# Two fused transformer blocks on one core: halved tiles and a leading VectorE tile around the second feed-forward block

## The chip, the cores and the metric

The kernel runs on one core of one Trainium2 chip. The metric is the device time of one execution in microseconds (us). Differences under about 0.2% (6.4 us) can't be told from no change with this kernel.

## The reference, cut to what matters

Two transformer blocks run one after the other over 1,024 tokens of width 1,024, all in f32. The second one ends so (the rest of both blocks isn't touched by the change):

```python
def rmsnorm(x, g):
    xf = x.astype(jnp.float32)
    y = xf * lax.rsqrt(jnp.mean(xf * xf, axis=-1, keepdims=True) + EPS)
    return (y * g.astype(jnp.float32)).astype(x.dtype)

def modulate(h, shift, scale):
    return h * (1 + scale) + shift

def swiglu(h, w_gu, w_down):
    a, b = jnp.split(h @ w_gu, 2, axis=-1)
    return (jax.nn.silu(a) * b) @ w_down

# in second_block; D_MODEL 1024, D_FF_2 2816
x = x + mx[2] * (jnp.concatenate([att_x, hg_x], axis=-1) @ w_out[l])
x = x + mx[5] * swiglu(modulate(rmsnorm(x, g_norm2[l]), mx[3], mx[4]), w_gu[l], w_down[l])
...
return rmsnorm(x, g_final)
```

## The kernel before

**Data.** Activations lie feature-major: `m["x"]` is 8 tiles (`KT`) of 128 features x 1,024 tokens. Every large product is split for accuracy: an operand is kept as a rounded high part (`b_hi` for activations, `whi` for weights) and a remainder (`b_lo`, `wlo`), and a product takes three matmuls: high x high, high x remainder, remainder x high. A matmul takes 512 tokens, so one input tile k into one output tile is 6 matmuls (`gemm_piece`, L512), and 48 for an output tile over all 8 input tiles. Four PSUM regions of 128 x 1,024 (`psl[0]` to `psl[3]`) are used: 0 to 2 in turn for outputs, 3 for column sums, and 2 also for the row of normalizing factors (the token row).

**Order.** Each engine runs its own program, in the written order, and waits on counters of named events: `up(name, ...)` marks an event and `at(name, ...)` waits for it. P, A, V and G are the counters of TensorE (PE), ScalarE (ACT), VectorE (DVE) and GpSimd (POOL). The counters `wh`, `ww` and `gm` say that a weight unit's high part is made, that its remainder is made, and that a unit's product is done. Weights are loaded by DMA from SP, rounded by ACT (L493) and subtracted by DVE (L501), three buffers of each.

**The stretch in question, stage "p".** `pe_project` makes the 8 output tiles of `w_out`. DVE adds each of them, times its gate, to the residual (L1486). ACT squares the new tile (L1433), POOL adds the squares of tiles 0 to 6 into `acc` (L1402), and `pe_stat` sums the columns of `acc` and then of the last square with a matrix of ones (L86). All engines then wait for those sums (`after_project`). Next, in `act_mlp` and `dve_mlp`, one more weight unit is split (L493, L501), DVE scales the sums (L1705), ACT takes the root (L1625), DVE the reciprocal (L1707), and PE turns the result into the token row by 8 transposes (`rows`, L79).

**The eight input tiles.** For each k in order, DVE makes z = x times the column factor times the token row (L1713), ACT adds the shift and rounds it to `b_hi` (L1632), and DVE makes the remainder `b_lo` (L1716). z has two buffers, the squares' buffers `m["sq"]`. PE waits for the event `l` k and then does 12 matmuls for that k: 6 for each of the first two units of `w_gu`. From the third unit on, PE has whole units of 48 matmuls. `mlp_plan` orders the 22 pairs of up tiles (`w_gu`) and the six groups of down tiles (L1604).

**Stage "d", the last group.** The same add (L1763), square and sum follow the last group of down tiles, which has two input tiles: 12 matmuls for each of 8 output tiles. Then `dve_last` scales (L2701), takes the reciprocal (L2703), and multiplies the eight tiles by gain and token row (L2707), and `sp_last` stores each of them to HBM (L2684).

Of the kernel before, what the change touches and what calls it, by code (L numbers as in the profile page):

```python
# [15 lines left out]
T = 1024  # L16
TC = 256
TA = T + TC
KT = 8
# [27 lines left out]
class Signal:  # L47
# [23 lines left out]
    def end(self):  # L71
        return self.sem, self.step if self.known is None else max(self.known.values())

# [255 lines left out]
class Kernel:  # L329
# [1024 lines left out]
    def after_project(self, e, sig):  # L1354
        e.wait_ge(*sig[0].at("cs", "p", KT - 1))
        e.wait_ge(*sig[1].at("sq", "p", KT - 1))
        e.wait_ge(*sig[2].at("add", KT - 1))
# [29 lines left out]
    def pe_stat(self, e, m, sig, tag):  # L1387

        P, A, V, G = sig
        e.wait_ge(*G.at("acc", tag, KT - 2))  # L1390
        col_sums(e, self.psl[3], m["acc"], self.con("ones"), True, False)
        e.wait_ge(*A.at("sq", tag, KT - 1))
        col_sums(e, self.psl[3], m["sq"][(KT - 1) % 2], self.con("ones"), False, True).then_inc(*P.up("cs", tag, KT - 1))
# [40 lines left out]

    def act_project(self, e, m, sig, name):
        P, A, V, G = sig
        j0 = UNIT[name, 0]
        for i in range(KT):
            if i:
                self.act_weights(e, j0 + i + 3)  # L1440
            if i:
                e.wait_ge(*V.at("add", i - 1))
                self.act_stat(e, m, sig, "p", i - 1, m["x"][:, i - 1, :])
        first = name == "dn_out"
        for k in range(KT - 1 if first else 0):
            e.wait_ge(*P.at("taken", k))
            self.act_plain(e, m, sig, k)
        e.wait_ge(*V.at("add", KT - 1))
        if first:
            e.wait_ge(*self.gm.at(j0 + KT - 1))  # L1450
            self.act_plain(e, m, sig, KT - 1)
        self.act_stat(e, m, sig, "p", KT - 1, m["x"][:, KT - 1, :])
        if not first:
            self.after_project(e, sig)
# [11 lines left out]
    def dve_project(self, e, m, sig, name, gate=None):  # L1466
        P, A, V, G = sig
        j0 = UNIT[name, 0]
        for i in range(KT):
# [13 lines left out]
            if gate is None:  # L1483
                e.tensor_tensor(x, x, ps, ALU.add).then_inc(*V.up("add", i))
            else:
                e.scalar_tensor_tensor(out=x, in0=ps, scalar=gate[i], in1=x, op0=ALU.mult,  # L1486
                                       op1=ALU.add).then_inc(*V.up("add", i))
# [43 lines left out]
    def pe_mlp(self, e, m, sig, n_ff, ring, up, down, beside=None):  # L1531
# [5 lines left out]
        def tokens():  # L1537
            e.wait_ge(*V.at("rc"))
            rows(e, self.psl[2], self.st[:, 0:8], self.con("ident")).then_inc(*P.up("rw"))

        if gated:
            tokens()
            for k in range(KT):
                e.wait_ge(*V.at("l", k))
                for part in range(2):
                    for i in range(2):
                        if k == 0 and part == 0:
                            e.wait_ge(*self.ww.at(j0 + i))
                        ins = self.gemm_piece(e, self.psl[i], j0 + i, k, part, self.b_hi, self.b_lo)
                        if k == KT - 1 and part == 1:  # L1550
                            ins.then_inc(*self.gm.up(j0 + i))
# [67 lines left out]
    def act_mlp(self, e, m, sig, n_ff, ring, up, down, shift=None, beside=None):  # L1619
# [6 lines left out]
        if shift is None:  # L1626
            e.wait_ge(*P.at("rw"))
            e.activation(m["row"], self.psl[2], ACT.Copy).then_inc(*A.up("row"))
        else:
            for k in range(KT):  # L1630
# [5 lines left out]
        for kind, f, n in mlp_plan(n_ff, ring):  # L1636
# [31 lines left out]
            else:  # L1668
                for i in range(8):
# [5 lines left out]
                    if f + n == n_ff and i:  # L1675
                        for k in (i - 1, 7) if i == 7 else (i - 1,):
                            e.wait_ge(*V.at("down", f, k))
# [20 lines left out]

    def dve_mlp(self, e, m, sig, n_ff, ring, up, down, wcol, shift=None, gate=None, beside=None):
# [8 lines left out]
        e.wait_ge(*P.at("rw") if gated else A.at("row"))  # L1708
        for k in range(KT if gated else 0):
            z = m["sq"][k % 2]  # L1710
            if k >= 2:
                e.wait_ge(*V.at("l", k - 2))
            e.scalar_tensor_tensor(out=z, in0=m["x"][:, k, :], scalar=wcol[:, k:k + 1], in1=self.psl[2],  # L1713
                                   op0=ALU.mult, op1=ALU.mult).then_inc(*V.up("z", k))
            e.wait_ge(*A.at("h", k))
            e.scalar_tensor_tensor(out=self.b_lo[:, k, :], in0=z, scalar=shift[:, k:k + 1],  # L1716
                                   in1=self.b_hi[:, k, :].bitcast(F32), op0=ALU.add, op1=ALU.subtract).then_inc(*V.up("l", k))
        j = j0 + 2
        before = {}
        for kind, f, n in mlp_plan(n_ff, ring):  # L1720
# [27 lines left out]
            else:  # L1748
                for i in range(8):
# [12 lines left out]
                    else:  # L1762
                        e.scalar_tensor_tensor(out=x, in0=ps, scalar=gate[i], in1=x, op0=ALU.mult,  # L1763
                                               op1=ALU.add).then_inc(*V.up("down", f, i))
# [915 lines left out]
    def sp_last(self, e):  # L2680
        V = self.mm2[2]
        for k in range(KT):
            e.wait_ge(*V.at("y", k))
            e.dma_start(self.out[:, k, :], self.x2[:, k, :]).then_inc(*self.outst.up(k))  # L2684
        e.wait_ge(*self.outst.end())

    def pe_last(self, e):
        P, A, V, G = self.mm2
        e.wait_ge(*V.at("rc2"))
        rows(e, self.psl[2], self.st[:, 0:8], self.con("ident")).then_inc(*P.up("rw2"))  # L2690
# [7 lines left out]
    def dve_last(self, e):  # L2698
# [5 lines left out]
        e.wait_ge(*P.at("rw2"))  # L2704
        for k in range(KT):
            x = self.x2[:, k, :]
            e.scalar_tensor_tensor(out=x, in0=x, scalar=self.par("gf")[:, k:k + 1], in1=self.psl[2], op0=ALU.mult,  # L2707
                                   op1=ALU.mult).then_inc(*V.up("y", k))

# [478 lines left out]
```

## Time and profile before

| | before |
|---|---|
| median of 3 runs | 3191.41 us (3189.16 to 3192.23) |
| the profiled execution, its own time | 3190.96 us |
| its span, first to last instruction | 3189.1 us |
| mean granted clock of PE, share of full | 0.987 |
| PE busy | 3046.8 us (96%) |
| DVE, ACT, POOL busy | 1543.6, 1000.1, 450.3 us (48%, 31%, 14%) |
| DMA, mean over the span | 58 GB/s |

The table says which engine is busy, and not which one sets the end of a stretch. For that the chain of waits and the timeline of the stretch are read. PE's clock is granted at one of two levels, 2.4 GHz (1.00 in the windows) and 1.2 GHz (0.50).

### The profile page before, as it was taken

How to read it: one execution, taken by the hardware profiler on the slowest of the kernel's cores; microseconds unless marked ns; L12 is line 12 of the kernel's file. 1: busy time of each engine (PE TensorE's matmuls, PEld its weight loads, DVE VectorE, ACT ScalarE, POOL GpSimd, SP SyncE). 2: the span in 40 equal slices, each digit the busy share in tenths (PEclk: the TensorE clock that was granted, in tenths of full speed). 3: DMA queues.
4: the chain of work that ended last, by engine and by line, in shares of the span. 5: the costliest groups of instructions: out<-in, count | busy, mean ns of one | idle time of the engine just before them, and what ended most of it. 6: DMA issues, size and time to landing. Idle time of an engine off the chain costs nothing.

```text
span 3189.1 us, 36113 instructions
## 1 busy us (share of the span) xinstructions
PE 3046.8 (96%) x14927; PEld 2487.1 (78%) x14927; DVE 1543.6 (48%) x1907; ACT 1000.1 (31%) x1441; POOL 450.3 (14%) x352
## 2 busy tenths in 40 slices
PE   8899999989999999999989999999898999999997
PEld 6688888878788888888866668888776888888886
DVE  7566666553565553433566764456644122222224
ACT  5555555552311122212423332233322111111111
POOL 4333333321000001000300002133300000000001
PEclk9999999999999999999999999999999999999999
DMA  3111111122233431111210001101131111111111
GB/s 124 40 47 47 47 47 47 47 67 99 65 115 121 129 120 52 49 51 47 94 54 7 9 10 48 34 21 40 47 112 31 56 47 47 52 47 47 50 43 60
DMA packets 77235, 184.75 MB, mean 58 GB/s; under 512 B 7056, under 2 KB 29072, under 8 KB 77072
## 3 DMA queue, kind: packets, MB, share of 16 engines
q1 hardware_dynamic: 77072, 182.44, 18.2%
q8 instruction: 119, 1.95, 0.3%
q14 instruction: 44, 0.36, 0.0%
HBM read 163.87 MB, written 15.79 MB: 56 GB/s over the span
## 4 chain that ended last, share of the span: by engine, by line
PE 86%; DVE 8%; ACT 4%; issue 2%; POOL 0%; DMA 0%; POOLq 0%; DVEq 0%; SPq 0%; ACTq 0%
PE ps L512 39%; PE ps L1604 18%; PE ps L2950 8%; PE ps L2291 4%; DVE b L2899 2%; PE ps L2429 1%; PE ps L909 1%; PE ps L2255 1%; PE ps L2284 1%; PE ps L2283 1%; DVE b L501 1%; PE ps L916 1%; ACT b L493 1%; PE ps L86 1%; PE ps L891 1%
## 5 line engine op out<-in xcount | busy, mean ns | idle before, releaser
L512 PE MATMUL ps<-b 128*128 128x512 f32 x6024 | 1494.9, 399 | 35.6 <-DVE b L501 14.0
L512 PEld LDWEIGHTS ps<-b 128*128 128x128 f32 x6024 | 1109.9, 190 | 251.2 <-issue 19.9
L1604 PE MATMUL ps<-b 128*128 128x512 f32 x2592 | 599.1, 392 | 0.7 <-DVE b L1745 0.7
L1604 PEld LDWEIGHTS ps<-b 128*128 128x128 f32 x2592 | 485.0, 187 | 109.3 <-DVE b L1745 1.1
L501 DVE TENSOR_TENSOR b<-b 128x1024 fp32r<-128x1024 f32 (+1 forms) x206 | 255.3, 1241 | 288.3 <-ACT b L493 280.9
L493 ACT ACTIVATE b<-b 128x1024 fp32r<-128x1024 f32 (+1 forms) x206 | 214.9, 1045 | 515.9 <-PE ps L1604 427.4
L2950 PE MATMUL ps<-b 128*128 128x512 f32 (+1 forms) x1464 | 327.3, 379 | 6.8 <-ACT b L3010 5.9
L2950 PEld LDWEIGHTS ps<-b 128*128 128x128 f32 x1464 | 255.0, 192 | 56.5 <-issue 11.5
L1402 POOL TENSOR_TENSOR b<-b 128x1024 f32<-128x1024 f32 x18 | 43.2, 2399 | 916.8 <-ACT b L1433 916.4
L2291 PE MATMUL ps<-b 128*128 128x512 f32 x320 | 163.0, 592 | 0.0
L1761 DVE TENSOR_TENSOR b<-b,ps 128x1024 f32<-128x1024 f32 x64 | 78.1, 1220 | 152.4 <-PE ps L1604 152.3
L2301 ACT ACTIVATE b<-ps 128x512 f32<-128x512 f32 x160 | 95.3, 597 | 149.7 <-PE ps L2284 149.7
L1763 DVE SCALAR_TENSOR_TENSOR b<-ps,b 128x1024 f32<-128x1024 f32 x48 | 61.6, 1283 | 150.2 <-PE ps L1604 150.2
L1665 ACT ACTIVATE b<-b 128x1024 fp32r<-128x1024 f32 x54 | 57.3, 1060 | 217.2 <-DVE b L1736 216.2
L2313 DVE TENSOR_REDUCE b<-ps 128x1 f32<-128x1280 f32 x64 | 95.1, 1488 | 42.7 <-PE ps L2255 42.3
L1661 ACT ACTIVATE b<-b 128x1024 f32<-128x1024 f32 x32 | 33.9, 1060 | 251.8 <-DVE b L1741 251.8
L1745 DVE TENSOR_TENSOR b<-b 128x1024 fp32r<-128x1024 f32 x54 | 66.2, 1225 | 95.8 <-ACT b L1665 95.8
L1741 DVE SCALAR_TENSOR_TENSOR b<-ps,b 128x1024 f32<-128x1024 f32 x32 | 39.2, 1224 | 148.1 <-PE ps L512 135.9
L1238 POOL TENSOR_TENSOR b<-b 128x256 f32<-128x256 f32 x96 | 82.7, 864 | 194.4 <-DVE b L1126 115.6
L1736 DVE TENSOR_TENSOR b<-b,ps 128x1024 f32<-128x1024 f32 x22 | 26.9, 1222 | 165.9 <-PE ps L512 162.2
L2899 DVE SCALAR_TENSOR_TENSOR b<-b 128x1024 f32<-128x1024 f32 x72 | 104.4, 1450 | 0.8
L2283 PE MATMUL ps<-b 128*128 128x512 f32 x160 | 98.5, 616 | 0.0
(306 smaller groups left out, 3292.8 us busy)
## 6 DMA issues: line engine op xcount, KB each, us to landing
b<-in_down SPq DMA_DIRECT2D x52, 512.0 KB, 3.7
b<-in_mod SPq DMA_DIRECT2D x96, 256.0 KB, 2.7
b<-in_gu SPq DMA_DIRECT2D x44, 512.0 KB, 3.6
b<-scratch SPq DMA_DIRECT2D x38, 512.0 KB, 4.4
b<-in_dn_in SPq DMA_DIRECT2D x32, 512.0 KB, 5.1
b<-in_up SPq DMA_DIRECT2D x32, 512.0 KB, 3.8
b<-in_win SPq DMA_DIRECT2D x26, 512.0 KB, 3.7
scratch<-b SPq DMA_DIRECT2D x18, 512.0 KB, 2.9
```

What stands on the lines that cost most here:

```text
L493: e.activation(self.whi[j % SPL][:, 0:cols], self.raw[j % RAW][:, 0:cols], ACT.Copy).then_inc(*self.wh.up(j))
L501: e.tensor_tensor(self.wlo[j % SPL][:, 0:cols], self.raw[j % RAW][:, 0:cols], self.whi[j % SPL][:, 0:cols].bitcast(F32), ALU.subtract).the ...
L512: ins = e.matmul(ps[:, c], w, h[:, k, c], start=first and k == 0 and i == 0, stop=last and k == KT - 1 and i == 2)
L1238: e.tensor_tensor(out, own, m.broadcast_to([128, 4, 64 >> lv, 1 << lv]), ALU.mult).then_inc(*G.up("m", h, lv, f))
L1604: ins = e.matmul(ps[:, c], w, u[:, at[k], c], start=k == 0 and p == 0, stop=k == n - 1 and p == 2)
L1761: e.tensor_tensor(x, x, ps, ALU.add).then_inc(*V.up("down", f, i))
L2283: e.matmul(S[t % 3], blk(self.ks[g], b), self.qs[g][:, :, qc], start=True, stop=False)
L2291: e.matmul(O[i % 2], self.vx[:, b, 64 * g:64 * g + 128], self.prob[(t - 2) % 4], start=b == 0, stop=b == 9).then_inc(*P.up("pv", t - 2))
L2301: e.activation(self.prob[t % 4], S[t % 3], ACT.Exp, scale=0.125).then_inc(*A.up("ex", t))
L2313: e.tensor_reduce(mx[:, j:j + 1], MX[1 if i else j % 2], AX.X, ALU.max).then_inc(*V.up("mx", i, j))
L2899: e.scalar_tensor_tensor(out=dst, in0=k.d_pad[c % 2][:, t:t + T], scalar=cw[:, t:t + 1], in1=dst, op0=ALU.mult, op1=ALU.add).then_inc(*V.u ...
L2950: ins = e.matmul(self.bank[p], (hi, hi, lo)[i], x, start=k == 0 and i == 0, stop=last)
```

## The change

`HALVES` are tokens 0 to 511 and 512 to 1,023. Outside the second feed-forward block and its two borders nothing changes. The first block's calls of the same helpers keep their form.

- The last residual tile, k = 7, of the stages "p" and "d" is added in two halves, squared in two halves (`act_stat_last`), and its column sums are two sets of four.
- The token row is made in two halves, each with its own event.
- Input tile 0 is made in halves throughout: z, high part, remainder, and PE's first 12 matmuls in two sets of six.
- In `dve_first_tiles`, DVE makes z for tile k + 1 ahead of the remainder of tile k, after a wait for the remainder of tile k - 1, which frees the buffer.
- At the end the token row is made in halves, the final multiplies of tiles 0 and 7 are halves, and tile 7 is stored as two DMAs.

The diff:

```diff
@@ -70,6 +70,10 @@
 
     def end(self):
         return self.sem, self.step if self.known is None else max(self.known.values())
+
+
+
+HALVES = (slice(0, 512), slice(512, 1024))
 
 
 def rows(e, ps, cols, ident):
@@ -1353,8 +1357,9 @@
 
     def after_project(self, e, sig):
         e.wait_ge(*sig[0].at("cs", "p", KT - 1))
-        e.wait_ge(*sig[1].at("sq", "p", KT - 1))
-        e.wait_ge(*sig[2].at("add", KT - 1))
+        half = [1] if sig is self.mm2 else []
+        e.wait_ge(*sig[1].at("sq", "p", KT - 1, *half))
+        e.wait_ge(*sig[2].at("add", KT - 1, *half))
 
     def pe_project(self, e, m, sig, name, free):
 
@@ -1389,8 +1394,15 @@
         P, A, V, G = sig
         e.wait_ge(*G.at("acc", tag, KT - 2))
         col_sums(e, self.psl[3], m["acc"], self.con("ones"), True, False)
-        e.wait_ge(*A.at("sq", tag, KT - 1))
-        col_sums(e, self.psl[3], m["sq"][(KT - 1) % 2], self.con("ones"), False, True).then_inc(*P.up("cs", tag, KT - 1))
+        sq = m["sq"][(KT - 1) % 2]
+        if m is self.m1:
+            e.wait_ge(*A.at("sq", tag, KT - 1))
+            col_sums(e, self.psl[3], sq, self.con("ones"), False, True).then_inc(*P.up("cs", tag, KT - 1))
+            return
+        for f, c in enumerate(HALVES):
+            e.wait_ge(*A.at("sq", tag, KT - 1, f))
+            ins = col_sums(e, self.psl[3][:, c], sq[:, c], self.con("ones"), False, True, 4)
+        ins.then_inc(*P.up("cs", tag, KT - 1))
 
     def pool_stat(self, e, m, sig, tag):
 
@@ -1431,6 +1443,15 @@
         if k >= 2:
             e.wait_ge(*G.at("acc", tag, max(1, k - 2)))
         e.activation(m["sq"][k % 2], x, ACT.Square).then_inc(*A.up("sq", tag, k))
+
+    def act_stat_last(self, e, m, sig, tag, made):
+
+        P, A, V, G = sig
+        k = KT - 1
+        e.wait_ge(*G.at("acc", tag, k - 2))
+        for f, c in enumerate(HALVES):
+            e.wait_ge(*made[f])
+            e.activation(m["sq"][k % 2][:, c], m["x"][:, k, c], ACT.Square).then_inc(*A.up("sq", tag, k, f))
 
     def act_project(self, e, m, sig, name):
         P, A, V, G = sig
@@ -1445,12 +1466,13 @@
         for k in range(KT - 1 if first else 0):
             e.wait_ge(*P.at("taken", k))
             self.act_plain(e, m, sig, k)
-        e.wait_ge(*V.at("add", KT - 1))
         if first:
+            e.wait_ge(*V.at("add", KT - 1))
             e.wait_ge(*self.gm.at(j0 + KT - 1))
             self.act_plain(e, m, sig, KT - 1)
-        self.act_stat(e, m, sig, "p", KT - 1, m["x"][:, KT - 1, :])
-        if not first:
+            self.act_stat(e, m, sig, "p", KT - 1, m["x"][:, KT - 1, :])
+        else:
+            self.act_stat_last(e, m, sig, "p", [V.at("add", KT - 1, f) for f in range(2)])
             self.after_project(e, sig)
 
     def act_plain(self, e, m, sig, k):
@@ -1483,8 +1505,9 @@
             if gate is None:
                 e.tensor_tensor(x, x, ps, ALU.add).then_inc(*V.up("add", i))
             else:
-                e.scalar_tensor_tensor(out=x, in0=ps, scalar=gate[i], in1=x, op0=ALU.mult,
-                                       op1=ALU.add).then_inc(*V.up("add", i))
+                for f, c in enumerate(HALVES if i == KT - 1 else [slice(0, T)]):
+                    e.scalar_tensor_tensor(out=x[:, c], in0=ps[:, c], scalar=gate[i], in1=x[:, c], op0=ALU.mult,
+                                           op1=ALU.add).then_inc(*V.up("add", i, *([f] if i == KT - 1 else [])))
         if gate is None:
             self.dve_plain(e, m, sig, KT - 1)
         else:
@@ -1536,16 +1559,23 @@
 
         def tokens():
             e.wait_ge(*V.at("rc"))
-            rows(e, self.psl[2], self.st[:, 0:8], self.con("ident")).then_inc(*P.up("rw"))
+            for f, c in enumerate(HALVES):
+                rows(e, self.psl[2][:, c], self.st[:, 4 * f:4 * f + 4], self.con("ident")).then_inc(*P.up("rw", f))
 
         if gated:
             tokens()
-            for k in range(KT):
+            for f, c in enumerate(HALVES):
+                e.wait_ge(*V.at("l", 0, f))
+                for i in range(2):
+                    if f == 0:
+                        e.wait_ge(*self.ww.at(j0 + i))
+                    a, b = blk(self.whi[(j0 + i) % SPL], 0), blk(self.wlo[(j0 + i) % SPL], 0)
+                    for w, h in ((a, self.b_hi), (a, self.b_lo), (b, self.b_hi)):
+                        e.matmul(self.psl[i][:, c], w, h[:, 0, c], start=w is a and h is self.b_hi, stop=False)
+            for k in range(1, KT):
                 e.wait_ge(*V.at("l", k))
                 for part in range(2):
                     for i in range(2):
-                        if k == 0 and part == 0:
-                            e.wait_ge(*self.ww.at(j0 + i))
                         ins = self.gemm_piece(e, self.psl[i], j0 + i, k, part, self.b_hi, self.b_lo)
                         if k == KT - 1 and part == 1:
                             ins.then_inc(*self.gm.up(j0 + i))
@@ -1624,10 +1654,13 @@
         e.wait_ge(*V.at("ms"))
         e.activation(self.st[:, 8:16], self.st[:, 0:8], ACT.Sqrt).then_inc(*A.up("rt"))
         if shift is None:
-            e.wait_ge(*P.at("rw"))
+            e.wait_ge(*P.at("rw", 1))
             e.activation(m["row"], self.psl[2], ACT.Copy).then_inc(*A.up("row"))
         else:
-            for k in range(KT):
+            for f, c in enumerate(HALVES):
+                e.wait_ge(*V.at("z", 0, f))
+                e.activation(self.b_hi[:, 0, c], m["sq"][0][:, c], ACT.Identity, bias=shift[:, 0:1]).then_inc(*A.up("h", 0, f))
+            for k in range(1, KT):
                 e.wait_ge(*V.at("z", k))
                 e.activation(self.b_hi[:, k, :], m["sq"][k % 2], ACT.Identity, bias=shift[:, k:k + 1]).then_inc(*A.up("h", k))
         group = self.mlp_group(n_ff, ring)
@@ -1674,6 +1707,9 @@
                         next(beside, None)
                     if f + n == n_ff and i:
                         for k in (i - 1, 7) if i == 7 else (i - 1,):
+                            if gated and k == KT - 1:
+                                self.act_stat_last(e, m, sig, "d", [V.at("down", f, k, half) for half in range(2)])
+                                continue
                             e.wait_ge(*V.at("down", f, k))
                             if gated:
                                 self.act_stat(e, m, sig, "d", k, m["x"][:, k, :])
@@ -1695,6 +1731,33 @@
             if kind == "down" and i == f:
                 return (n + m) % 3
             n += (2 if gated else 1) if kind == "up" else 8
+
+    def dve_first_tiles(self, e, m, sig, wcol, shift):
+
+        P, A, V, G = sig
+
+        def tile(k, c):
+            return e.scalar_tensor_tensor(out=m["sq"][k % 2][:, c], in0=m["x"][:, k, c], scalar=wcol[:, k:k + 1],
+                                          in1=self.psl[2][:, c], op0=ALU.mult, op1=ALU.mult)
+
+        def low(k, c):
+            return e.scalar_tensor_tensor(out=self.b_lo[:, k, c], in0=m["sq"][k % 2][:, c], scalar=shift[:, k:k + 1],
+                                          in1=self.b_hi[:, k, c].bitcast(F32), op0=ALU.add, op1=ALU.subtract)
+
+        for f, c in enumerate(HALVES):
+            e.wait_ge(*P.at("rw", f))
+            tile(0, c).then_inc(*V.up("z", 0, f))
+        for f, c in enumerate(HALVES):
+            e.wait_ge(*A.at("h", 0, f))
+            low(0, c).then_inc(*V.up("l", 0, f))
+            if f == 0:
+                tile(1, slice(0, T)).then_inc(*V.up("z", 1))
+        for k in range(1, KT):
+            if k + 1 < KT:
+                e.wait_ge(*V.at("l", k - 1, *([1] if k == 1 else [])))
+                tile(k + 1, slice(0, T)).then_inc(*V.up("z", k + 1))
+            e.wait_ge(*A.at("h", k))
+            low(k, slice(0, T)).then_inc(*V.up("l", k))
 
     def dve_mlp(self, e, m, sig, n_ff, ring, up, down, wcol, shift=None, gate=None, beside=None):
         P, A, V, G = sig
@@ -1705,16 +1768,10 @@
         e.tensor_scalar(self.st[:, 0:8], self.psl[3][:, 0:1024:128], 1.0 / D, EPS, ALU.mult, ALU.add).then_inc(*V.up("ms"))
         e.wait_ge(*A.at("rt"))
         e.reciprocal(self.st[:, 0:8], self.st[:, 8:16]).then_inc(*V.up("rc"))
-        e.wait_ge(*P.at("rw") if gated else A.at("row"))
-        for k in range(KT if gated else 0):
-            z = m["sq"][k % 2]
-            if k >= 2:
-                e.wait_ge(*V.at("l", k - 2))
-            e.scalar_tensor_tensor(out=z, in0=m["x"][:, k, :], scalar=wcol[:, k:k + 1], in1=self.psl[2],
-                                   op0=ALU.mult, op1=ALU.mult).then_inc(*V.up("z", k))
-            e.wait_ge(*A.at("h", k))
-            e.scalar_tensor_tensor(out=self.b_lo[:, k, :], in0=z, scalar=shift[:, k:k + 1],
-                                   in1=self.b_hi[:, k, :].bitcast(F32), op0=ALU.add, op1=ALU.subtract).then_inc(*V.up("l", k))
+        if gated:
+            self.dve_first_tiles(e, m, sig, wcol, shift)
+        else:
+            e.wait_ge(*A.at("row"))
         j = j0 + 2
         before = {}
         for kind, f, n in mlp_plan(n_ff, ring):
@@ -1760,8 +1817,10 @@
                     if gate is None:
                         e.tensor_tensor(x, x, ps, ALU.add).then_inc(*V.up("down", f, i))
                     else:
-                        e.scalar_tensor_tensor(out=x, in0=ps, scalar=gate[i], in1=x, op0=ALU.mult,
-                                               op1=ALU.add).then_inc(*V.up("down", f, i))
+                        halves = f + n == n_ff and i == KT - 1
+                        for half, c in enumerate(HALVES if halves else [slice(0, T)]):
+                            e.scalar_tensor_tensor(out=x[:, c], in0=ps[:, c], scalar=gate[i], in1=x[:, c], op0=ALU.mult,
+                                                   op1=ALU.add).then_inc(*V.up("down", f, i, *([half] if halves else [])))
                     if beside:
                         next(beside, None)
 
@@ -2680,14 +2739,16 @@
     def sp_last(self, e):
         V = self.mm2[2]
         for k in range(KT):
-            e.wait_ge(*V.at("y", k))
-            e.dma_start(self.out[:, k, :], self.x2[:, k, :]).then_inc(*self.outst.up(k))
+            for f, c in enumerate(HALVES if k == KT - 1 else [slice(0, T)]):
+                e.wait_ge(*V.at("y", k, f))
+                e.dma_start(self.out[:, k, c], self.x2[:, k, c]).then_inc(*self.outst.up(k, f))
         e.wait_ge(*self.outst.end())
 
     def pe_last(self, e):
         P, A, V, G = self.mm2
         e.wait_ge(*V.at("rc2"))
-        rows(e, self.psl[2], self.st[:, 0:8], self.con("ident")).then_inc(*P.up("rw2"))
+        for f, c in enumerate(HALVES):
+            rows(e, self.psl[2][:, c], self.st[:, 4 * f:4 * f + 4], self.con("ident")).then_inc(*P.up("rw2", f))
 
     def act_last(self, e):
         P, A, V, G = self.mm2
@@ -2701,12 +2762,15 @@
         e.tensor_scalar(self.st[:, 0:8], self.psl[3][:, 0:1024:128], 1.0 / D, EPS, ALU.mult, ALU.add).then_inc(*V.up("ms2"))
         e.wait_ge(*A.at("rt2"))
         e.reciprocal(self.st[:, 0:8], self.st[:, 8:16]).then_inc(*V.up("rc2"))
-        e.wait_ge(*P.at("rw2"))
         for k in range(KT):
-            x = self.x2[:, k, :]
-            e.scalar_tensor_tensor(out=x, in0=x, scalar=self.par("gf")[:, k:k + 1], in1=self.psl[2], op0=ALU.mult,
-                                   op1=ALU.mult).then_inc(*V.up("y", k))
-
+            for f, c in enumerate(HALVES if k in (0, KT - 1) else [slice(0, T)]):
+                if k == 0:
+                    e.wait_ge(*P.at("rw2", f))
+                x = self.x2[:, k, c]
+                ins = e.scalar_tensor_tensor(out=x, in0=x, scalar=self.par("gf")[:, k:k + 1], in1=self.psl[2][:, c], op0=ALU.mult,
+                                             op1=ALU.mult)
+                if k or f:
+                    ins.then_inc(*V.up("y", k, f if k else 0))
 
 
     def sync_program(self, e):
```

## Rows read from the trace of the kernel before

**Rows 1.** The page's chain that ended last, shares of the span by engine

```profile
PE 86%; DVE 8%; ACT 4%; issue 2%; POOL 0%; DMA 0%; POOLq 0%; DVEq 0%; SPq 0%; ACTq 0%
```

**Rows 2.** Chain from stage "p" on: start us, us, engine and line

```profile
2425.09 2.07 PE ps L86 x16
...
2430.20 1.10 PE ps L79 x8
...
2435.11 1.20 DVE b L1713
...
2436.33 1.16 ACT b L1632
...
2437.51 1.28 DVE b L1716
2438.80 1.20 DVE b L1713
...
2461.04 111.82 PE ps L512 x492
...
2617.66 87.06 PE ps L512 x384
```

**Rows 3.** Timeline of the same stretch; in brackets the idle time before

```profile
2422.39 1.95 PE L86 MATMUL ps<-b 128*128 128x128 f32 x16
2422.66 1.28 DVE L1486 SCALAR_TENSOR_TENSOR b<-ps,b 128x1024 f32<-128x1024 f32 x1 [7.27 <-PE ps L512]
...
2431.33 1.28 DVE L1713 SCALAR_TENSOR_TENSOR b<-b,ps 128x1024 f32<-128x1024 f32 x1 [1.18 <-PE ps L79]
...
2435.16 10.41 PE L512 MATMUL ps<-b 128*128 128x512 f32 x36 [3.87 <-DVE b L1716]
...
2468.20 2.35 DVE L501 TENSOR_TENSOR b<-b 128x1024 fp32r<-128x1024 f32 x2
```

**Rows 4.** Windows: busy us (count) of PE, PEld, DVE, ACT, POOL; clock; DMA

```profile
2431.70:2435.16 3.46, 0.00 (x0) 0.00 (x1) 2.24 (x3) 1.15 (x1) 0.00 (x0) 0.51 0.22 90
2435.16:2438.50 3.34, 3.34 (x8) 2.66 (x9) 2.12 (x2) 1.15 (x1) 0.00 (x0) 0.50 0.00 0
...
688.50:694.00 5.50, 5.18 (x16) 4.22 (x17) 2.30 (x5) 0.93 (x3) 0.72 (x1) 0.50 0.66 186
854.50:858.30 3.80, 3.49 (x8) 2.79 (x9) 2.53 (x3) 1.21 (x2) 0.00 (x0) 0.55 0.66 185
2350.50:2356.50 6.00, 5.85 (x18) 5.01 (x19) 1.91 (x3) 0.60 (x1) 0.00 (x0) 0.50 0.59 202
```

**Rows 5.** Groups by shape, half tiles of the stage before: busy us, mean ns

```profile
L2659 DVE SCALAR_TENSOR_TENSOR b<-b 128x512 f32<-128x512 f32 x2 | 1.5, 751 | 0.1
L1338 ACT ACTIVATE b<-b 128x512 fp32r<-128x512 f32 x2 | 1.3, 630 | 3.7 <-DVE b L2659 3.7
```

**Rows 6.** Timeline of DVE: L1486 waits for DVE's own L1476

```profile
2355.82 1.28 DVE L1476 SCALAR_TENSOR_TENSOR b<-b,ps 128x1024 f32<-128x1024 f32 x1 [3.99 <-DMA b<-scratch]
2357.14 1.28 DVE L1486 SCALAR_TENSOR_TENSOR b<-ps,b 128x1024 f32<-128x1024 f32 x1
```

**Rows 7.** Timeline of stage "d" and the end

```profile
3167.20 2.35 POOL L1402 TENSOR_TENSOR b<-b 128x1024 f32<-128x1024 f32 x1 [0.34 <-ACT b L1433]
...
3168.86 1.06 ACT L1433 ACTIVATE b<-b 128x1024 f32<-128x1024 f32 x1 [1.74 <-DVE b L1763]
...
3169.60 3.84 PE L86 MATMUL ps<-b 128*128 128x128 f32 x32 [2.09 <-POOL b L1402]
...
3174.18 1.09 PE L79 MATMUL ps<-b 128*128 128x128 f32 x8 [0.74 <-DVE b L2703]
3175.30 9.62 DVE L2707 SCALAR_TENSOR_TENSOR b<-b,ps 128x1024 f32<-128x1024 f32 x8 [1.18 <-PE ps L79]
3176.61 8.67 SPq L2684 DMA_DIRECT2D out<-b  x8
```

**Rows 8.** Window of the last stores, columns as in rows 4

```profile
3177.50:3187.50 10.00, 0.00 (x0) 0.00 (x0) 7.42 (x7) 0.00 (x0) 0.00 (x0) 0.59 1.02 405
```

## The prediction

> **What bounds the kernel now.** I read four views in this order. The page's chain of waits says that PE is the chain for 86% of the span, DVE for 8% and ACT for 4% [rows 1]. So an edit to DVE or ACT is worth something only where the chain leaves PE, and the change touches three such places.
>
> The chain in order of time shows the first two [rows 2]. At 2425.09 PE starts its last column sums, which take 2.07 us, to 2427.16. At 2430.20 the token row starts, and then a ladder begins: DVE makes z, ACT the high part, DVE the remainder, and the next z starts where the last one did plus 3.69 us (2435.11 to 2438.80). PE is in the chain again only from 2461.04. From there it has no break: 384 matmuls in 87.06 us are 0.2267 us each, so the 12 for one input tile take 2.72 us. PE needs 2.72, the ladder gives a tile every 3.69, and PE idles for the difference. The timeline shows which engine had been ready: PE had finished the first sums at 2424.34 (2422.39 + 1.95) and waited for the last square [rows 3].
>
> The third place is the end. There the timeline shows POOL's last sum ending at 3169.55, PE's 32 matmul records following without a gap, and the stores trailing the final multiplies [rows 7]. The windows show the stores running at 405 GB/s with the DMA engines full [rows 8].
>
> **Part 1, stage "p" by halves.** A half add costs 0.75 alone and a half square about 0.63, from the half tiles of the stage before [rows 5]. A whole op starts 1.20 after a whole op in front of it though it lasts 1.28 [rows 2], so I let a second half start 0.67 after the first. First half: 2422.66 + 0.75 + 0.63 + two handovers of 0.03 gives 2424.10. PE is in the first sums until 2424.34, so it doesn't wait. Second half: the add ends at 2422.66 + 0.67 + 0.75 = 2424.08, the square at 2424.74, and PE wants it near 2425.3. PE thus runs all 32 records in one piece. Stage "d" has that piece: 3.84 us [rows 7]. 2422.39 + 3.84 = 2426.23 against 2427.16 is **0.93 us gained**. If the pipeline has to fill twice (1.95 + 2.05) it is 0.77. The way from the sums to the token row (3.04 us) has the same instructions as before and moves with it.
>
> **Part 2, the eight tiles.** I count from the start of the token row, which was 2430.20. Before, PE took up tile 7 at 2461.04, or 30.84, and left it at 30.84 + 2.72 = **33.56**. For the changed order:
>
> - Eight transposes take 1.09 and z starts at 1.13 [rows 2, 3, 7]. Four end half of 1.09 sooner, near 0.58, and z starts at 0.62.
> - z half 0 ends at 1.37, half 1 starts at 1.28 and ends at 2.03. A half high part I put at 0.72 (0.63 plus the 0.09 by which a whole one, 1.16, exceeds a whole square, 1.06) [rows 2, 5, 7]. The halves end at 2.11 and 2.83.
> - Remainder half 0 ends at 2.13 + 0.75 = 2.88, and PE starts at 2.94. z of tile 1 starts at 2.79, remainder half 1 at 3.99, ends 4.74. PE is busy with half 0 until about then at full clock, longer at the lower one.
> - z of tile 2 waits for that remainder and starts at 4.77, remainder 1 at 5.97, and ends at 7.25. PE can start tile 1 at 7.31.
> - From there DVE's period is a z that waited for DVE's own last result and a remainder behind it: 1.32 (2355.82 to 2357.14) [rows 6] plus 1.20 is 2.52 us. ACT's 1.16 lies beside DVE's remainder. 2.52 is under PE's 2.72, so PE sets the pace.
>
> If PE's clock were full, the end would be 7.31 + 7 x 2.72 = 26.35. But PE starts at the lower level. Before, it fell to 0.50 about 4.5 us after the sums and stayed there for the first 3.34 us of work; a matmul then took 3.34 / 8 = 0.42 us [rows 4]. The ladder hid that, since tile 0 had 3.69 us of slack behind it and every next tile 0.97 more. Now nothing hides it beyond the wait for tile 1. With C us of work at the lower level the end is 2.94 + 96 x 0.2267 + C x (1 - 0.2267 / 0.42) = 24.70 + 0.46 C, and never below 26.35. Four stretches of dense work show C: 3.34, 3.4 (3.8 us at a mean of 0.55), 5.5 and 6.0 [rows 4]. I take their mean, 4.6, because where the clock rises within new work can't be read from a stretch that starts elsewhere. The end is 26.8, and the gain **33.56 - 26.8 = 6.76 us**, with 7.21 at C = 3.3 and 6.10 at C = 6.0.
>
> The Trainium skill, "TensorE: Matmul & The Clock Gate", Part 1, says that the clock is low by default, is released by sustained work, and that the same kernel can show different counts of slow matmuls from run to run. The four stretches agree as far as they go. Its durations for 512 columns, 426.7 and 215.7 ns, would make the factor 0.49 in place of 0.46 and the end, by an estimate, 0.15 us later.
>
> Behind tile 7 nothing else is due. The fourth unit's remainder was ready at 2469.4 (first of the two at 2468.20) [rows 3], while PE asks for it one unit of 48 matmuls after 2463.76, at 2474.6. That split hangs on the first unit's product, so it moves with PE and keeps its 5.2 us. SP's weight loads keep their order and their waits.
>
> **Part 3, stage "d" by halves.** I cost it at nothing. The last square ended at 3169.92, and PE began only at 3169.60, when POOL was done, with 1.92 us of other sums first [rows 7]. The cover for the two extra half instructions is that 1.6 us. Without it an extra half pair would cost 0.1 to 0.2.
>
> **Part 4, the end.** z of tile 0 starts at 3174.18 + 0.62 = 3174.80 in place of 3175.30. Its second half ends at 3174.80 + 0.66 + 0.75 = 3176.21, where the whole tile ended at 3176.58. The first store goes out 0.37 sooner. From there the stores set the end: 8 tiles are 4.19 MB, at 405 GB/s 10.4 us [rows 8], while DVE needs 9.62 for all eight tiles [rows 7], so they fall behind DVE and the end follows the first store. **0.37 us gained.** Halving the last store moves no bytes off the queue. I bound its effect by minus 0.2 (a ninth issue; eight spanned 8.67 us) and plus 0.65 (half of one tile's 1.3 us, if the queue were empty), and take 0.
>
> The Trainium skill, "DMA: Bandwidth & Descriptors", Rules for kernel authors, advises against splitting a transfer in two, because both parts use the same 16 engines. It speaks of partition halves and these are column halves; the full engines in the window agree. Its "Perfetto Trace Analysis", DMA Optimizations, expects splitting to help when the engines are idle, which would give the 0.65.
>
> **Sum.** 0.93 + 6.76 + 0 + 0.37 = 8.06 us. Against the profiled execution's own time, 3190.96, that is 3182.90. The median of the runs is 0.45 above it, so 3183.4, or 0.25% faster.
>
> **Rivals.**
>
> - *The clock stays low.* If short waits between tiles kept PE at the lower level through all 96 matmuls, the end would be 2.94 + 96 x 0.42 = 43.3, 9.7 later than before, and the total 3191.4 + 9.7 - 1.3 = 3199.8. It decides from C = 22 us of work on. Against it: in this same stretch the clock rose after 3.34 us of work, at a lower density of work than is to come, and the longest low stretch of dense work is 6.0 [rows 4]. Chance 0.03. The same page of the Trainium skill warns, in its section on HAM oscillation, of matmul bursts between waits that leave the clock low each time; the ladder of before doesn't show it.
> - *DVE's lead doesn't come about,* because the wait for its own remainder or the shared buffers put z, high part and remainder in a row again. Then tile 7 is ready at 7.25 + 6 x 3.69 = 29.39, PE ends it at 32.17, and the gain is 1.39 + 0.93 + 0.37 = 2.7: 3188.7. From a period of 2.80 on, DVE would be the bound. For it: each z does wait for DVE's own result. Against it: that wait is in rows 6 and costs 0.12. Chance 0.07.
> - *Only the eight tiles bring anything, and at the slow end:* the borders are swallowed by another wait and C is 6.0. Then 6.1 are gained: 3185.3. For it: in both borders the first consumer is a queue or a pooled sum that another engine feeds. Chance 0.08.
> - *Nothing gained or a small loss elsewhere,* for example from code that now lies otherwise in a program of 3,100 other microseconds: 3191. Nothing in the rows speaks for it. Chance 0.02.
>
> **How the numbers follow.** The forecast has 0.80. Its own working spans 0.77 + 6.10 + 0.17 = 7.0 to 0.93 + 7.21 + 1.02 = 9.2 us, or 3182.2 to 3184.4. The runs of before lie 2.3 below to 0.8 above their median. Together that is 3181 to 3186; I set the upper end at 3186.5 for the third rival. The line for "faster" is 3185.0. Most of the forecast's 0.80 is above that gain, with 0.02 more from the third rival: 0.79. Slower has the first rival's 0.03. The rest, 0.18, is within 0.2%.
>
> **What would show it.** In stage "p" PE's sums are one piece of 32 records of about 3.84 us. The ladder's chain goes from DVE and ACT to PE after tile 1, DVE's z starts lie about 2.7 apart (held by nothing but its own order, 2.5), and the 96 matmuls take 24 to 25 us from first to last. In stage "d" the sums still follow POOL. The last store lands 0.4 us sooner relative to the sums. The prediction is wrong if PE shows waits between tiles 2 to 7, if the clock is low for over 8 us of work, or if a wait appears at the third or fourth unit.

## The result and the profile after

| | before | changed |
|---|---|---|
| median of 17 runs each | 3192.31 us (3189.16 to 3196.28) | 3183.52 us (3180.83 to 3189.33) |
| ratio, with 95% interval | | 0.9975 (0.9969 to 0.9982) |
| profiled span | 3189.1 us | 3180.9 us |

The changed kernel is 0.25% faster; the interval, 0.18 to 0.31%, begins just under the 0.2% that count. The forecast was 3183.4 us. The kernel before came out at 3192.31, 0.9 us above the median of three runs, 3191.41, from which the forecast had started. The 17 runs of each kernel fall into a lower and an upper group: ten and seven of before (to 3192.8, from 3194.8), twelve and five of the changed one (to 3184.4, from 3187.8), and the means are 8.1 us apart in the lower group and 7.0 in the upper one.

The chain of waits of the changed kernel, from stage "p" on (start in us, duration in us, engine and line; x32 is a count of instructions):

```profile
2421.10 3.70 PE ps L90 x32
...
2426.01 1.22 DVE b L505
...
2427.84 1.98 PE ps L83 x8
...
2429.85 0.75 DVE b L1740
2430.60 0.70 DVE b L1744
...
2431.34 5.49 PE ps L1574 x12
2436.83 128.07 PE ps L516 x564
```

In [rows 2] DVE and ACT carried the chain for all eight tiles. Now they carry it for less than one: from 2431.34 on the chain is PE without a break. The column sums (x32) are one piece. Two things stand out: the token row took 1.98 us, where before it took 1.10, and the first 12 matmuls took 5.49, where 12 take 2.72 at the full clock.

The timeline of the same stretch shows why DVE left the chain:

```profile
2420.93 3.85 PE L90 MATMUL ps<-b 128*128 128x128 f32 x32
2421.20 1.41 DVE L1509 SCALAR_TENSOR_TENSOR b<-ps,b 128x512 f32<-128x512 f32 x2 [7.27 <-PE ps L516]
...
2431.34 5.49 PE L1574 MATMUL ps<-b 128*128 128x512 f32 x12 [1.53 <-DVE b L1744]
...
2435.69 1.28 DVE L1740 SCALAR_TENSOR_TENSOR b<-b,ps 128x1024 f32<-128x1024 f32 x1
...
2436.89 1.28 DVE L1744 SCALAR_TENSOR_TENSOR b<-b 128x1024 fp32r<-128x1024 f32 x1
2437.00 1.15 ACT L1665 ACTIVATE b<-b 128x1024 fp32r<-128x1024 f32 x1 [1.36 <-DVE b L1740]
2438.20 1.28 DVE L1740 SCALAR_TENSOR_TENSOR b<-b,ps 128x1024 f32<-128x1024 f32 x1
...
2455.68 1.03 ACT L1688 ACTIVATE b<-ps 128x1024 f32<-128x1024 f32 x1 [4.50 <-PE ps L516]
```

One z (L1740) starts 2.51 us after the one before, and ACT's high part (L1665) lies beside DVE's remainder (L1744). No z or remainder has an idle time in front of it. The last line is the first activation of the block. In all ten profiles it starts 0.03 us before the last matmul of tile 7 does. Reckoned as the forecast did it, by 12 x 0.2267 from PE's first matmul for tile 7, the end of tile 7 was 2463.76 in the kernel before and its activation started at 2463.65. So I use this start as the mark in all kernels, and add 0.11 us where I compare with the forecast.

The windows give the reason for 1.98 and 5.49 (columns as in [rows 4]):

```profile
2424.80:2426.90 2.10, 0.00 (x0) 0.00 (x0) 0.89 (x1) 1.06 (x1) 0.00 (x0) 0.98 0.40 115
2426.90:2431.34 4.44, 1.97 (x8) 1.57 (x8) 2.85 (x7) 1.64 (x3) 0.00 (x0) 0.50 0.52 182
2431.34:2437.00 5.66, 5.66 (x13) 4.47 (x14) 5.59 (x6) 2.31 (x3) 0.00 (x0) 0.50 0.00 0
2437.10:2439.00 1.90, 1.90 (x10) 1.54 (x9) 1.86 (x2) 1.06 (x1) 0.00 (x0) 1.00 0.00 0
```

PE's clock fell to 0.50 at 2426.8, two microseconds after the sums. So it was low under the whole token row, and through the first 5.7 us of matmuls.

Stage "d" and the end, on the timeline, answering to [rows 7]:

```profile
3159.23 2.35 POOL L1414 TENSOR_TENSOR b<-b 128x1024 f32<-128x1024 f32 x1 [0.34 <-ACT b L1445]
...
3160.42 1.23 ACT L1454 ACTIVATE b<-b 128x512 f32<-128x512 f32 x2 [1.27 <-DVE b L1822]
3161.63 3.84 PE L90 MATMUL ps<-b 128*128 128x128 f32 x32 [2.10 <-POOL b L1414]
...
3166.21 1.09 PE L83 MATMUL ps<-b 128*128 128x128 f32 x8 [0.74 <-DVE b L2764]
```

POOL releases the sums as before, and the halved squares end at 3161.65, 1.9 us before PE has done its first sixteen sums and comes to them.

**Where the 8.2 us of span went.** I cut both spans at five marks:

| stretch | before | changed | difference |
|---|---|---|---|
| start to the column sums of "p" | 2422.39 | 2420.93 | 1.46 |
| sums to token row | 7.81 | 6.91 | 0.90 |
| token row to first activation | 33.45 | 27.84 | 5.61 |
| first activation to sums of "d" | 705.95 | 705.95 | 0 |
| sums of "d" to last token row | 4.58 | 4.58 | 0 |
| last token row to end of span | 14.92 | 14.69 | 0.23 |

The change itself is worth 6.74 us in this pair. The other 1.46 us come from stages whose instructions are the same in both. The spans are known to 0.1 us, so the last row can be off by 0.05.

### The profile page after: what moved, and what is told of

It is laid out like the page before. It is cut to its first block, busy times and chain, and to the rows that moved or that the text cites. A ratio compares the mean times of both kernels' runs of the same rounds, so it can differ in the third digit from the quotient of the medians.

```text
span 3180.9 us, 36123 instructions
## 1 busy us (share of the span) xinstructions
PE 3044.1 (96%) x14927; PEld 2486.9 (78%) x14927; DVE 1545.2 (49%) x1913; ACT 1001.1 (31%) x1444; POOL 451.3 (14%) x352
## 4 chain that ended last, share of the span: by engine, by line
PE 86%; DVE 7%; ACT 4%; issue 2%; POOL 0%; DMA 0%; POOLq 0%; DVEq 0%; SPq 0%; ACTq 0%
PE ps L516 39%; PE ps L1634 18%; PE ps L3014 8%; PE ps L2350 4%; DVE b L2963 2%; PE ps L2488 1%; PE ps L913 1%; PE ps L2314 1%; PE ps L2343 1%; PE ps L2342 1%; DVE b L505 1%; PE ps L920 1%; PE ps L90 1%; ACT b L497 1%; PE ps L895 1%
## 5 line engine op out<-in xcount | busy, mean ns | idle before, releaser
L1822 DVE SCALAR_TENSOR_TENSOR b<-ps,b 128x1024 f32<-128x1024 f32 (+1 forms) x49 | 61.7, 1261 | 150.2 <-PE ps L1634 150.2
L1798 DVE SCALAR_TENSOR_TENSOR b<-ps,b 128x1024 f32<-128x1024 f32 x32 | 39.2, 1224 | 147.9 <-PE ps L516 135.7
```

## The experiments

Eight kernels were run in two groups, each beside the kernel before. Five of them have one run only, and one total can't tell a part of the change from noise. So the verdicts rest on the stretches, which repeat to 0.05 us where the clock is the same (the last column, rounded as above, to 0.1). No kernel had stage "d" and the end changed alone, so what is said of them is by elimination. C is the time in us for which PE worked at the lower clock from its first matmul for tile 0 on; "hidden" means that the tiles came so slowly that this cost nothing.

| kernel | start of sums | sums to token row | token row to first activation | C | last row to end |
|---|---|---|---|---|---|
| before | 2422.39 | 7.81 | 33.45 | 3.4, hidden | 14.92 |
| changed | 2420.93 | 6.91 | 27.84 | 5.7 | 14.69 |
| lead_alone | 2423.29 | 7.81 | 28.19 | 3.4 | 14.94 |
| tile0_halves_alone | 2427.15 | 7.81 | 32.16 | hidden | 14.93 |
| stage_d_store_whole | 2420.76 | 6.91 | 27.55 | 6.1 | 14.65 |
| pe_kept_busy | 2425.42 | 6.92 | 26.32 | 0 | 14.71 |
| stage_p_alone | 2420.95 | 6.90 | 34.32 | hidden | 15.00 |
| before_kept_busy | 2424.88 | 7.81 | 33.46 | 0 | 14.92 |
| changed_again | 2420.24 | 6.91 | 26.96 | 4.9 | 14.66 |
| busy_in_both_stages | 2421.87 | 6.92 | 26.33 | 0 | 14.71 |

From the first activation to the sums of "d" it was 705.95 to 706.00 in all ten.

**lead_alone.** Against the kernel before:

```diff
+        tile(0, whole).then_inc(*V.up("z", 0))
+        tile(1, whole).then_inc(*V.up("z", 1))
+        low(0, whole)                      # after the high part of tile 0
         for k in range(1, KT):
-            if k >= 2: e.wait_ge(*V.at("l", k - 2))
-            tile(k, whole).then_inc(*V.up("z", k))
+            if k + 1 < KT:
+                e.wait_ge(*V.at("l", k - 1))
+                tile(k + 1, whole).then_inc(*V.up("z", k + 1))
             e.wait_ge(*A.at("h", k))
             low(k, whole).then_inc(*V.up("l", k))
```

> Only DVE's order is changed: z of tile k + 1 ahead of the remainder of tile k, all tiles whole, nothing halved anywhere. My theory: DVE's period falls from 3.69 to 2.51 us, PE starts tile 0 at 4.95 us after the token row (as before) and becomes the bound; from the token row to the end of tile 7 it takes 26.7 + 0.46 C, with C us of work at the lower clock, so 28.2 to 29.5 in place of 33.56: 4 to 5.3 us gained, the largest part of the change. The rival (the halves of tile 0 carry the gain, and the wait for the own remainder keeps the ladder) expects 32 or more.

Its timeline (the line numbers are those of its own kernel, here and below):

```profile
2431.10 1.09 PE L85 MATMUL ps<-b 128*128 128x128 f32 x8 [3.06 <-DVE b L1804]
...
2436.06 6.20 PE L518 MATMUL ps<-b 128*128 128x512 f32 x19 [3.88 <-DVE b L1763]
...
2438.55 1.28 DVE L1759 SCALAR_TENSOR_TENSOR b<-b,ps 128x1024 f32<-128x1024 f32 x1
...
2441.06 1.28 DVE L1759 SCALAR_TENSOR_TENSOR b<-b,ps 128x1024 f32<-128x1024 f32 x1
...
2459.29 1.03 ACT L1707 ACTIVATE b<-ps 128x1024 f32<-128x1024 f32 x1 [5.55 <-PE ps L518]
```

PE starts 4.96 after the token row, the z's are 2.51 apart, and the stretch is 28.19 (28.30 to the end of tile 7). The forecast's formula gives 26.7 + 0.46 x 3.4 = 28.3. The order of DVE alone is worth 5.26 us. The rival, which expected 32 or more, falls.

**tile0_halves_alone.** The kernel before with only the token row and tile 0 by halves. DVE's order is the old one for tiles 1 to 7, as this part of the diff against the changed kernel shows:

```diff
         for k in range(1, KT):
-            if k + 1 < KT:
-                e.wait_ge(*V.at("l", k - 1, *([1] if k == 1 else [])))
-                tile(k + 1, slice(0, T)).then_inc(*V.up("z", k + 1))
+            if k >= 2:
+                e.wait_ge(*V.at("l", k - 2, *([1] if k == 2 else [])))
+            tile(k, slice(0, T)).then_inc(*V.up("z", k))
```

> Only the token row and tile 0 are halved (z, high part, remainder, PE's first twelve matmuls); the ladder for tiles 1 to 7 is the old one. My theory: the ladder keeps its 3.69 us per tile and starts about 1.3 us sooner, so the way from the token row to the end of tile 7 is 32.3 us in place of 33.56, and the lower clock costs nothing. The rival (halves carry the gain) expects 28 or less.

```profile
2445.90 1.27 DVE L1759 SCALAR_TENSOR_TENSOR b<-b,ps 128x1024 f32<-128x1024 f32 x1
...
2449.60 1.27 DVE L1759 SCALAR_TENSOR_TENSOR b<-b,ps 128x1024 f32<-128x1024 f32 x1
```

The timeline has the old 3.70 us from z to z, and the stretch is 32.16: 1.29 gained, and the rival, 28 or less, falls. The two parts add to 6.55. Together they gave 5.6 to 6.5 in the three profiles without idle matmuls, and 33.45 - 26.32 = 7.13 at full clock.

**stage_d_store_whole.** The changed kernel with these two edits undone:

```diff
-                        halves = f + n == n_ff and i == KT - 1
+                        halves = False       # and act_stat whole for k = 7
-            for f, c in enumerate(HALVES if k in (0, KT - 1) else [slice(0, T)]):
+            for f, c in enumerate(HALVES if k == 0 else [slice(0, T)]):
```

> The changed kernel with stage d whole again and the last tile multiplied and stored whole; the last token row and the first tile's final multiply stay halved. My theory: neither mattered. From the first activation of the second feed-forward block to the start of the last sums it takes 705.95 us, as in both kernels, and from the last token row to the end of the span 14.7, as in the changed one. The rival (the halved last store brings the 0.2 us at the end) expects 14.9 as before the change; if the halved square helped, the sums would start 0.2 or more later.

```profile
3160.43 1.06 ACT L1447 ACTIVATE b<-b 128x1024 f32<-128x1024 f32 x1 [1.74 <-DVE b L1856]
3161.17 3.84 PE L92 MATMUL ps<-b 128*128 128x128 f32 x32 [2.10 <-POOL b L1416]
```

The whole square ends at 3161.49, after PE has begun the sums but before it gets to this square, and the sums keep their place and length. The end is 14.65 against 14.69. Neither half brought anything, so the gain at the end is left to the halved token row and first multiply. The stores bear this out:

```profile
3166.44 9.75 DVE L2805 SCALAR_TENSOR_TENSOR b<-b,ps 128x512 f32<-128x512 f32 x9 [0.74 <-PE ps L85]
3167.87 8.68 SPq L2778 DMA_DIRECT2D out<-b  x8
```

The eight stores went out over 8.68 us, as before (8.67), but began 2.12 us after the token row's start at 3165.75, where it was 2.43.

**pe_kept_busy.** The changed kernel with 18 matmuls whose result is overwritten:

```diff
         if gated:
+            self.pe_warm(e, j0, 11)      # 128x512 matmuls of a weight tile into psl[0]
             tokens()
+            self.pe_warm(e, j0, 7)
```

> The changed kernel with 18 idle matmuls on PE, whose result is overwritten: 11 between the sums and the token row, 7 between the token row and tile 0, both in time in which PE waits. My theory: the lower clock is what the changed kernel lost against my forecast, in the token row (1.97 us in place of 1.09) and in the first matmuls. With PE at work the clock stays at 1.00, the token row takes 1.1, and from its start to the end of tile 7 it is 26.4 us in place of 27.95: about 1.5 us off the total, 0.05% against the changed kernel, 0.3% against the one before. The rival (tile 7's end is set by DVE's period and the clock is beside the point) expects 27.9 again.

Timeline and one window:

```profile
2429.03 2.79 PE L1566 MATMUL ps<-b 128*128 128x512 f32 x11
...
2432.34 1.09 PE L85 MATMUL ps<-b 128*128 128x128 f32 x8 [0.52 <-DVE b L1804]
...
2435.37 1.66 PE L1591 MATMUL ps<-b 128*128 128x512 f32 x6 [0.33 <-DVE b L1763]
...
2458.66 1.03 ACT L1707 ACTIVATE b<-ps 128x1024 f32<-128x1024 f32 x1 [3.46 <-PE ps L518]
```

```profile
2430.00:2435.00 5.00, 4.48 (x23) 3.19 (x22) 3.34 (x6) 1.78 (x4) 0.00 (x0) 1.00 0.65 210
```

The clock stays at 1.00, the first six matmuls take 1.66, and the stretch is 26.32 in place of 27.84: 1.52 us, as expected. The ratio of the totals to the kernel before was 0.9976 (0.9966 to 0.9986; ten runs), so the expected 0.05% against the changed kernel isn't seen there. This profile reached the sums at 2425.42, 4.5 us later than the changed one, for a reason that lies ahead of the edit (last section).

**stage_p_alone.** Against the kernel before:

```diff
-                e.scalar_tensor_tensor(out=x, in0=ps, ...).then_inc(*V.up("add", i))
+                for f, c in enumerate(HALVES if i == KT - 1 else [slice(0, T)]): ...
-        self.act_stat(e, m, sig, "p", KT - 1, m["x"][:, KT - 1, :])
+        self.act_stat_last(e, m, sig, "p", [V.at("add", KT - 1, f) for f in range(2)])
```

> Only the add, the square and the column sums of the last residual tile of stage p are halved; all else is as before. My theory: from the start of the column sums to the token row it is 6.9 us in place of 7.81, and from the token row to the first activation of the block (0.1 us before the end of tile 7) 33.45 as before, whatever the clock does. The rival (the weight unit between the sums and the token row takes up the gain) expects 7.8.

```profile
2420.95 3.85 PE L92 MATMUL ps<-b 128*128 128x128 f32 x32
2427.85 1.97 PE L85 MATMUL ps<-b 128*128 128x128 f32 x8 [3.06 <-DVE b L1810]
...
2462.17 1.03 ACT L1713 ACTIVATE b<-ps 128x1024 f32<-128x1024 f32 x1 [1.29 <-PE ps L518]
```

The first half of the expectation came true: 6.90. The second didn't: 34.32, not 33.45. The token row itself ran at the lower clock, 1.97 in place of 1.09, and nothing hides that, since all later work waits for it. "Whatever the clock does" was wrong for this one piece, in the old order too.

**before_kept_busy.** The kernel before with `pe_warm` of 11 and 15 in the same two places.

> The kernel before with idle matmuls on PE, 11 between the sums and the token row and 15 between the token row and tile 0, which keep the clock at 1.00. My theory: the old ladder hid the lower clock, so nothing is gained: 33.45 us from the token row to the first activation. The rival (the lower clock cost the kernel before about as much as the changed one, so that it was no cost of the change) expects about 32.

```profile
2432.69 1.09 PE L85 MATMUL ps<-b 128*128 128x128 f32 x8 [0.53 <-DVE b L1810]
...
2466.15 1.03 ACT L1713 ACTIVATE b<-ps 128x1024 f32<-128x1024 f32 x1 [1.30 <-PE ps L518]
```

It took 33.46 against 33.45, and the rival, about 32, falls. The old ladder did hide the lower clock of the matmuls; there it became a cost only with the new order. In the token row it costs in either order.

**changed_again** and **busy_in_both_stages.** The first is the changed kernel once more. The second has 11 and 7 idle matmuls in stage "p" and these in stage "d":

```diff
+                        e.wait_ge(*V.at("down", f, 5))   # its PSUM region has been read
+                        for _ in range(7):
+                            e.matmul(ps[:, 0:512], blk(w, 0), w[:, 0:512], start=True, stop=True)
                         self.pe_stat(e, m, sig, "d")
```

> The changed kernel once more, beside the next one on the same chip. My theory: 6.91 us from the sums to the token row; from there to the first activation 26.3 if the clock is full, 27.5 to 28.4 if it is low at tile 0; 705.95 to the sums of stage d; 14.7 at the end; ratio to the kernel before 0.9975. A rival, that the forecast total was met by the clock of earlier stages and the change itself is worth 6.7 us, expects 0.9979.

> The changed kernel with idle matmuls in both stages: 11 and 7 around the token row, and 7 between PE's last down product and the column sums of stage d, where PE waits for POOL. My theory: tile 7 ends 26.4 us after the token row, and the 32 sum records of stage d always take 3.84 us (two of six profiles so far show 5.47, with the clock at 0.50): 1.5 us less than the changed kernel plus 0.5 on the mean, ratio to the kernel before 0.9969. The rival (PE must not be given work there, since the idle matmuls hold up the sums) expects the sums to start 0.2 us or more later after POOL.

The timeline of changed_again:

```profile
2427.15 1.09 PE L83 MATMUL ps<-b 128*128 128x128 f32 x8 [3.06 <-DVE b L1770]
2430.18 5.30 PE L1574 MATMUL ps<-b 128*128 128x512 f32 x12 [1.94 <-DVE b L1744]
...
2454.11 1.03 ACT L1688 ACTIVATE b<-ps 128x1024 f32<-128x1024 f32 x1 [4.11 <-PE ps L516]
```

| | median | ratio to before, 95% |
|---|---|---|
| changed_again | 3183.36 us, 7 runs | 0.9972 (0.9961 to 0.9984) |
| busy_in_both_stages | 3182.22 us, 5 runs | 0.9965 (0.9953 to 0.9978) |

The changed kernel's total repeated, 3183.36 after 3183.52. Its token row ran at the full clock this time, and the stretch was 26.96 us at C = 4.9, below the 27.5 to 28.4 that I expected for a low clock. The expected ratio 0.9975 and the rival's 0.9979 both lie in its interval, so only the stretches can tell them apart. busy_in_both_stages beats the kernel before and has the shorter stretch, 26.33. Its last sums still start 0.05 us after POOL's last sum ends (3161.12 after 3161.07), so the rival falls. That its total is below the changed kernel's isn't shown, since the intervals overlap, nor is the saving in stage "d": the changed kernel's two profiles had the full clock there. Where it was low, in lead_alone and in tile0_halves_alone, the sums took this:

```profile
3165.25 5.47 PE L92 MATMUL ps<-b 128*128 128x128 f32 x32 [2.10 <-POOL b L1416]
```

## Why the prediction was right, and where it was off

- **What bounds the stretch: right.** DVE's new period was 2.51 (2.52 forecast), PE's 2.72 set the pace, and the rival in which the lead doesn't come about is refuted by lead_alone. Of the 6.74 us in the profiled pair, 5.61 are in the eight tiles, and the 96 matmuls took 24.45 us, as forecast (24 to 25). One sign was misread: DVE's z starts lie 2.51 apart, not the 2.7 I named, because nothing makes DVE wait for PE.
- **Part 1: right.** 0.89 to 0.91 in every kernel that has it, against 0.93; the second half was ready in time.
- **Part 2: the formula right, one term short.** The start of PE, 2.94 us after the token row, was 3.03 in every kernel with tile 0 halved and a full-clock token row. The first z began 0.69 us after the row's start (2427.84 against 2427.15 in changed_again), and not 0.62: half a token row came later than I took it. The formula, start + 21.76 + 0.46 C, gives 27.9, 28.3, 27.6 and 27.05 for the end of tile 7 in changed, lead_alone, stage_d_store_whole and changed_again; measured were 27.95, 28.30, 27.66 and 27.07. With the clock full it was 26.43, where 26.35 was the floor. What failed is the size of the clock's term. C was 4.9 to 6.1 in the three profiles of kernels with the new stretch and no idle matmuls, against the 4.6 I took. In one of them the low clock reached the token row, which the sum didn't hold at all (0.88 us more for the row, of which 0.47 came through to PE's start). The forecast gain of 6.76 was 5.6, 5.9 and 6.5.
- **Part 3: right,** at nothing.
- **Part 4: right in kind,** 0.21 to 0.27 against 0.37. z of tile 0 began at 0.69 after the row and not at 0.62, so the first store left 2.12 after the token row, 0.31 sooner than before and not 0.37; in stage_d_store_whole 0.27 of that came through. The halved store brought nothing, as the full DMA engines of [rows 8] had suggested.
- **The sum.** By stretches the change is worth 6.7, 7.1 and 7.7 us in the three profiles, 7.2 on the mean, and not 8.06; 6.7 lies under the 7.0 at the low end of the forecast's own working. There is one profile of the kernel before to compare with, and its token row had the full clock. The medians differ by 8.8, and the ratio gives 8.0 with an interval from 5.7 to 9.9. That the forecast total was met to 0.1 us is therefore luck: the gain by stretches fell short by 0.4 to 1.3 us, and stages ahead of the change scatter by more than that.
- **The clock that stays low,** the rival on the other side, needed 22 us of work; the longest was 6.1.

## What to carry to other kernels

Where engines hand tiles to each other in turn, compare the period at which tiles come with what the consumer needs for one, before halving anything. Here one reordering on DVE took the period from 3.70 to 2.51 us, under PE's 2.72, and gave four times what the halved first tile gave. When a stretch stops being bound by waits, costs that the waits hid come due, here PE's lower clock. Look for them in the windows of the old profile and add them to the sum. Halving a producer gave nothing where another engine held the consumer back (stage "d"), and neither did halving a transfer on full DMA engines.

## What the runs showed of the hardware

The place where the clock falls and rises isn't fixed by the program. Without idle matmuls before it, the token row starts 3.06 us after PE's last sum in seven profiles; it ran at full clock in five (1.09) and at the lower one in two (1.97). Two profiles of one kernel, changed and changed_again, differ so. The 32 sums of stage "d" took 3.84 in eight profiles and 5.47 in two. Idle matmuls in the gap kept the clock at 1.00 in all three kernels that had them.

I hadn't expected how far this reaches. With the same instructions ahead of it, the start of the sums in stage "p" lay between 2420.24 and 2427.15. The largest step is near 1,600 us, in the projections of the second block. The timeline of PE in the kernel before, then in tile0_halves_alone, then a window of each:

```profile
1599.80 1.64 PE L2950 MATMUL ps<-b 128*128 128x512 f32 x6
1601.28 1.84 PE L2074 MATMUL ps<-b 128*128 128x2 f32 x16
```

```profile
1599.88 2.71 PE L3049 MATMUL ps<-b 128*128 128x512 f32 x6
1602.38 3.41 PE L2167 MATMUL ps<-b 128*128 128x2 f32 x16
```

```profile
1602.00:1609.00 7.00, 7.00 (x34) 5.27 (x34) 3.72 (x6) 0.22 (x1) 0.00 (x0) 1.00 0.02 6
```

```profile
1602.00:1609.00 7.00, 7.00 (x25) 6.01 (x24) 1.12 (x3) 0.22 (x1) 0.00 (x0) 0.50 0.02 5
```

The clock was at 0.50 there in one profile and at 1.00 in the other, and the next block of matmuls began at 1610.67 in place of 1605.76. The same window of pe_kept_busy is at 0.50 too:

```profile
1602.00:1609.00 7.00, 7.00 (x26) 6.23 (x25) 1.40 (x4) 0.22 (x1) 0.00 (x0) 0.50 0.12 49
```

These are the two profiles that reached the sums of stage "p" last, at 2427.15 and 2425.42. A single total of this kernel can thus be several us off for a reason that has nothing to do with the edit. Why the clock falls in one execution and not in the next wasn't tried.
